# Expert loop of an encoder block: small matmuls gathered in two places, weight rows dealt to partitions in another order

## The chip, the cores and the metric

One NeuronCore of a Trainium2 chip runs the whole kernel; the other cores are idle. The metric is the device time of one execution in microseconds (us). Engines are named as in the profile: PE is TensorE's matmul, PEld its weight load, DVE VectorE, ACT ScalarE, POOL GpSimd, SP SyncE, which issues most of the DMAs.

## The reference, cut to what matters

One encoder layer over 512 tokens of 1024 features in float32: two attention branches, a gated merge, and then a mixture of experts, which is where the change lies. Each token goes to 4 of 32 experts:

```python
def run_block(args):
    xb, e = args
    gu = xb @ w_gate_up[e] + b_gate_up[e]
    return clamped_swiglu(gu) @ w_down[e] + b_down[e]

gate, up = gu[..., :D_FF], gu[..., D_FF:]
gate = jnp.minimum(gate, 7.0)
up = jnp.clip(up, -7.0, 7.0)
hidden = (up + 1.0) * (gate * jax.nn.sigmoid(1.702 * gate))
```

`xb` holds up to 128 tokens of one expert, `w_gate_up[e]` is 1024 x 2048 and `w_down[e]` 1024 x 1024, so an expert has 12 MB of weights. The results are weighted with the router's gates and added to the tokens' rows.

## The kernel before, in words

The attention part and the router take the first 470 us and are not touched, and so are the last norm and the stores. From there the kernel goes through *items*: one item is one expert with up to 128 rows (there are 32 items here). An item's weights come in 12 *chunks* of 1 MB: chunks 0 to 3 are the gate columns, 4 to 7 the up columns, 8 to 11 the down matrix, each chunk 256 rows of 1024 numbers. `expert_src` (line 295) lays the 256 rows on 128 partitions, two to a partition. Before the change partition p holds rows 2p and 2p+1.

float32 products are made from two rounded parts: ACT copies a chunk to its high part (`ex_split_hi`, line 656), DVE subtracts to get the low part in the chunk's own place (`ex_split_lo`, line 1032), and TensorE makes three products for each pair (`mm_split`, line 1172): high by high (line 1174), high by low and low by high (1175, 1176). One chunk is 12 matmuls of 128x512 (`weigh`, line 1413).

All engines run hand-written orders, linked by semaphores:

- SP (lines 378 to 387) loads a chunk of the next item as soon as `ex_used` says that its place has been read by TensorE.
- ACT (`act_item`, line 767) splits chunks, copies y out of PSUM with the router's weight (`rows_out`, line 757, sets `y_ready`), copies the transposed rows (`rows_hi`) and hidden values (`hidden_hi`), turns the slot products into row numbers (`index`, line 709, sets `f5_ready`), and makes the sigmoid (line 746).
- DVE (`dve_item`, line 1121) makes the one-hot rows for the slots (`serve`), the low parts, the clip of the up sum (line 1133) and the hidden values (line 1137).
- POOL (lines 492 to 502) gathers the next rows `xg` from HBM once `xt_ps` says that the last ones were transposed, and adds finished rows to `sum_rows`.
- TensorE (`pe_item`, line 1447) makes, in this order: up chunks 4 and 5, the transposes of the next item's rows (`rows_in`, line 1397), up chunks 6 and 7, the up bias; then gate chunk 0 of the next item, the slot products (`slots`, line 1386), chunk 1, the transposes of the hidden values (`hidden_T`, line 1405), chunks 2 and 3, the gate bias, the down bias; and down chunks 8 to 11.

A bias is a matmul of a bf16 table with a 0/1 column (`add_bias`, line 1425), two per bias. A slot product is four bf16 matmuls of 128x5. A transpose is a matmul with the data as weights and an identity as the moving operand, eight per item and kind. Because partition p holds rows 2p and 2p+1, the transposes must read every second column:

```python
last = t_.transpose(ps[:, 6 + k // 4, (k % 4) * CAP:(k % 4 + 1) * CAP],
                    xg[:, (k // 2) * 256 + k % 2:(k // 2 + 1) * 256:2], ident[0:CAP, 0:CAP])
```

Of the kernel before, what the change touches and what calls it, by code (L numbers as in the profile page):

```python
# [24 lines left out]
E, FF, TOPK = 32, 1024, 4  # L25
CAP = 128
# [8 lines left out]
def encoder_block(nc, x, g_mix, w_in, qa_norm, ka_norm, sink_b, w_branch_a, w_branch_b, w_out, g_ffn, w_router,  # L35
# [9 lines left out]
    with ctx:  # L45
# [3 lines left out]
        def sem(name):  # L49
            return ctx.enter_context(nc.semaphore(name))  # L50
# [44 lines left out]
        bias_tab = at("bias_tab", 190, [128, 3 * D], BF16)  # L95
# [6 lines left out]
        XT = at("XT", 96, [128, 2, KD, CAP], F32R)  # L102
# [12 lines left out]
        ident = sb("ident", [128, 128])  # L115
# [142 lines left out]
        xt_ps = sem("xt_ps")  # L258
        xt_hi = sem("xt_hi")
        xt_lo = sem("xt_lo")  # L260
        gate_ps = sem("gate_ps")
        up_ps = sem("up_ps")
        sig_done = sem("sig_done")
        glu_ready = sem("glu_ready")
        clip_ready = sem("clip_ready")
# [29 lines left out]
        def expert_src(e, c):  # L295

            q = c % 4
            if c < 8:
                w = w_gate_up[0, e, q * 256:(q + 1) * 256, (c // 4) * FF:(c // 4 + 1) * FF]
            else:  # L300
                w = w_down[0, e, q * 256:(q + 1) * 256, :]
            return w.rearrange("(p k) n -> p k n", k=2)

        def load_expert(sp, c, e):
            sp.dma_start(chunk[c][:, :].rearrange("p (k n) -> p k n", k=2), expert_src(e, c)).then_inc(expert_in[c], 16)
# [2 lines left out]
        def order(i, c, nxt):  # L308

            q = c - 4 if c in range(4, 8) else c + 4 if c < 4 else c if nxt else c - 4  # L310
            return 12 * i + 4 + q
# [194 lines left out]
        def _(act):  # L506
# [236 lines left out]
            first_split_hi(5)  # L743
            for c in (6, 7):
                ex_split_hi(0, c)
            def sigmoid(n):
                act.wait_ge(gate_ps, n)
                a.activation(sg, ps[0:CAP, 0:2, :].rearrange("p t n -> p (t n)"), ACT.Sigmoid,
                             scale=1.702).then_inc(sig_done, 1)

            a.activation(warm[:, :], eps[:, :], ACT.Sigmoid)
            sigmoid(1)
            act.wait_ge(items_ready, 1)
            last_item = act.value_load(items_i[0:1, 1:2], min_val=E - 1, max_val=E * PASSES - 1)
            act.sem_inc(y_ready, 1)
# [11 lines left out]
            def act_item(i, nxt, before=True):  # L767

                if nxt:
                    ex_split_hi(i + 1, 0)  # L770
                    ex_split_hi(i + 1, 1)
                if before:
                    rows_out(i - 1, 12 * i + 6)
                if nxt:
                    ex_split_hi(i + 1, 2)
                    rows_hi(i + 2, 0)
                    ex_split_hi(i + 1, 3)
                ex_split_hi(i, 8, nxt)
                if nxt:
                    act.wait_ge(ex_used, 12 * i + 10)  # L780
                    rows_hi(i + 2, 1)
                ex_split_hi(i, 9, nxt)
                if nxt:
                    act.wait_ge(scattered, 16 * i + ADDED)
                    index(i + 3, bass.ds((i + 3) % 4, 1))
                ex_split_hi(i, 10, nxt)
                hidden_hi(i + 1)
                ex_split_hi(i, 11, nxt)
                if nxt:
                    a.activation(warm[:, :], eps[:, :], ACT.Sigmoid)  # L790
                    ex_split_hi(i + 1, 4)
                    ex_split_hi(i + 1, 5)
                    sigmoid(i + 2)
                    ex_split_hi(i + 1, 6)
                    ex_split_hi(i + 1, 7)

# [17 lines left out]
        def _(dve):  # L814
# [306 lines left out]
            def dve_item(i, nxt):  # L1121

                if nxt:
                    dve.wait_ge(idx_done, i + 3)
                    serve(i + 3)
                    for c in range(3):
                        ex_split_lo(i + 1, c)
                    rows_lo(i + 2, 0)
                    ex_split_lo(i + 1, 3)
                else:  # L1130
                    ex_split_lo(i, 8, nxt)
                dve.wait_ge(up_ps, i + 1)
                v.tensor_scalar(hid, ps[0:CAP, 2:4, :].rearrange("p t n -> p (t n)"), 8.0, -6.0, ALU.min,  # L1133
                                ALU.max).then_inc(clip_ready, 1)
                dve.wait_ge(clip_ready, i + 1)
                dve.wait_ge(glu_ready, i + 1)
                v.scalar_tensor_tensor(out=hid, in0=sg, scalar=SILU_TOP, in1=hid, op0=ALU.min,
                                       op1=ALU.mult).then_inc(hid_ready, 1)
                if nxt:
                    rows_lo(i + 2, 1)  # L1140
                    ex_split_lo(i, 8, nxt)
                ex_split_lo(i, 9, nxt)
                hidden_lo(i + 1)
                ex_split_lo(i, 10, nxt)
                ex_split_lo(i, 11, nxt)
                if nxt:
                    ex_split_lo(i + 1, 4)
                    ex_split_lo(i + 1, 5)
                    glu(i + 2)
                    ex_split_lo(i + 1, 6)  # L1150
                    ex_split_lo(i + 1, 7)
# [16 lines left out]
        def _(pe):  # L1168
# [228 lines left out]
            def rows_in(n):  # L1397

                pe.wait_ge(gathered, n * 16)
                for k in range(KD):  # L1400
                    last = t_.transpose(ps[:, 6 + k // 4, (k % 4) * CAP:(k % 4 + 1) * CAP],  # L1401
                                        xg[:, (k // 2) * 256 + k % 2:(k // 2 + 1) * 256:2], ident[0:CAP, 0:CAP])
                last.then_inc(xt_ps, 1)

            def hidden_T(n):

                pe.wait_ge(hid_ready, n)
                for k in range(KD):
                    last = t_.transpose(ps[:, 6 + k // 4, (k % 4) * CAP:(k % 4 + 1) * CAP],  # L1409
                                        hid[:, (k // 2) * 256 + k % 2:(k // 2 + 1) * 256:2], ident[0:CAP, 0:CAP])  # L1410
                last.then_inc(hidT_ps, 1)

            def weigh(at, c, h, src, bank, fresh):

                pe.wait_ge(ex_lo, at + 1)
                q = c % 4
                for k in range(2):
                    for t in range(2):
                        last = mm_split(ps[0:CAP, bank + t, :], lambda p: src[:, p, 2 * q + k, :],
                                        lambda p: expert_w(c, h, p, k, t),  # L1420
                                        start=(fresh and q == 0 and k == 0), stop=(not fresh and q == 3 and k == 1))
                last.then_inc(ex_used, 1)
                return last

            def add_bias(e, bank, part, start):

                for t in range(2):
                    col = part * FF + t * 512
                    last = mm(ps[0:CAP, bank + t, :], pick[:, bass.ds(e, 1)].to_broadcast([128, CAP]),  # L1429
                              bias_tab[:, col:col + 512], start=start, stop=not start)  # L1430
                return last

            slots(0)
            slots(1)
# [2 lines left out]
            rows_in(1)  # L1437
            pe.wait_ge(xt_lo, 2)
            for c in range(4):
                weigh(c, c, c, XT, 0, True)  # L1440
            pe.wait_ge(bias_back, 16)
            pe.wait_ge(pick_set, 1)
            add_bias(0, 0, 0, False).then_inc(gate_ps, 1)
            pe.wait_ge(items_ready, 1)
            last_item = pe.value_load(items_i[0:1, 1:2], min_val=E - 1, max_val=E * PASSES - 1)

            def pe_item(i, nxt):

                for c in range(4, 8):
                    if c == 6:  # L1450
                        if nxt:
                            rows_in(i + 2)
                        else:
                            pe.wait_ge(gathered, (i + 2) * 16)
                            pe.sem_inc(xt_ps, 1)
                    weigh(order(i, c, nxt), c, hi_slot(c, nxt), XT, 2, True)
                add_bias(i % E, 2, 1, False).then_inc(up_ps, 1)
                if nxt:
                    pe.wait_ge(glu_ready, i + 1)
                    for c in range(4):  # L1460
                        if c == 0:
                            pe.wait_ge(xt_lo, 2 * i + 3)
                        weigh(order(i, c, nxt), c, hi_slot(c, nxt), XT, 0, True)
                        if c == 0:
                            pe.wait_ge(y_ready, i + 1)
                            slots(i + 3)
                        if c == 1:
                            pe.wait_ge(xt_lo, 2 * i + 4)
                            hidden_T(i + 1)
                    add_bias((i + 1) % E, 0, 0, False).then_inc(gate_ps, 1)  # L1470
                    pe.wait_ge(f5_ready, i + 4)
                else:
                    hidden_T(i + 1)
                    pe.wait_ge(y_ready, i + 1)
                add_bias(i % E, 4, 2, True)
                pe.wait_ge(hidT_lo, i + 1)
                for c in range(8, 12):
                    weigh(order(i, c, nxt), c, hi_slot(c, nxt), hidT, 4, False)

            with pe.Fori(0, last_item) as i:  # L1480
                pe_item(i, True)
# [40 lines left out]
```

## Time and profile before

| what | us |
|---|---|
| median of 3 runs | 1666.46 (1664.6 to 1666.61) |
| the profiled execution, whole | 1666.04 |
| its span in the profile | 1664.3 |
| TensorE busy in the span | 1597.3 (96%) |
| DVE busy | 1310.5 (79%) |
| ACT busy | 1074.0 (65%) |
| mean granted clock of TensorE | 0.98 of full speed |
| moved by DMA | 476.58 MB, 286 GB/s over the span |

The profile shows one execution. Matmuls overlap one another, so the duration of one (0.39 us for 128x512) is longer than the distance between two starts. Times in rows are us from the start of the span. "Landing" is the time from the issue of a DMA to the arrival of its last byte.

### The profile page before, as it was taken

The page shows a single profiled execution, that of the slowest core. Times are in us where ns is not written, and L with a number is a line of the kernel's source. Part 1 is how long each engine was busy: PE and PEld are TensorE (multiplying, and loading weights), DVE is VectorE, ACT ScalarE, POOL GpSimd, SP SyncE. Part 2 cuts the span into 40 slices and gives each one's busy share as a digit, 9 for nine tenths or more (in the row PEclk, how much of TensorE's full clock was granted, in tenths as well). Part 3 has the DMA queues.
Part 4 walks back from the last instruction along what each step waited for, and adds up shares of the span by engine and source line. Part 5 has one row for each costly group of instructions (what it writes and reads, how often), then busy time and mean ns, then how long its engine had stood idle before and what let it go on. Part 6 is the DMA issues. An engine that isn't in the chain of part 4 may idle for free.

```text
span 1664.3 us, 21630 instructions
## 1 busy us (share of the span) xinstructions
PE 1597.3 (96%) x7527; PEld 1266.9 (76%) x7527; DVE 1310.5 (79%) x1016; ACT 1074.0 (65%) x1113; POOL 145.5 (9%) x113
## 2 busy tenths in 40 slices
PE   7999899999969999999999999999999999999993
PEld 6788555678858888888888888888888888888882
DVE  4465464545579999998999999899999889999973
ACT  5243343422367777777777777777777777777762
POOL 6500000000010000010000001000000100000010
PEclk9999899999979999999999999999999999999997
DMA  8332000004489999999999999999999999999973
GB/s 289 120 102 76 16 1 1 1 26 177 149 343 357 381 380 381 380 373 356 381 380 381 380 380 368 362 380 381 379 383 381 360 367 382 379 381 382 378 250 126
DMA packets 114382, 476.58 MB, mean 286 GB/s; under 512 B 9704, under 2 KB 10224, under 8 KB 97872
## 3 DMA queue, kind: packets, MB, share of 16 engines
q1 hardware_dynamic: 100528, 432.83, 68.1%
q0 software_dynamic: 10224, 37.62, 8.8%
q10 hardware_dynamic: 3600, 5.73, 1.0%
q8 instruction: 19, 0.31, 0.1%
q14 instruction: 11, 0.09, 0.0%
HBM read 451.24 MB, written 24.90 MB: 286 GB/s over the span
## 4 chain that ended last, share of the span: by engine, by line
PE 94%; DVE 3%; DMA 1%; ACT 1%; issue 0%; ACTq 0%; SPq 0%; DVEq 0%; POOLq 0%
PE ps L1174 26%; PE ps L1176 26%; PE ps L1175 26%; PE ps L1429 3%; PE ps L1269 2%; PE ps L1245 2%; PE ps L1401 2%; PE ps L1409 2%; PE ps L1282 2%; PE ps L1249 1%; PE ps L1289 1%; DVE mx L898 1%; DVE split L839 1%; PE ps L1353 0%; DMA xs<-in_x 0%
## 5 line engine op out<-in xcount | busy, mean ns | idle before, releaser
L1036 DVE TENSOR_TENSOR chunk_lo<-chunk,chunk_hi 128x2048 fp32r<-128x2048 f32 x384 | 861.7, 2284 | 56.7 <-ACT chunk_hi L660 54.0
L660 ACT ACTIVATE chunk_hi<-chunk 128x2048 fp32r<-128x2048 f32 x378 | 722.9, 1914 | 136.5 <-PE ps L1176 135.5
L1174 PE MATMUL ps<-chunk_hi,XT 128*128 128x512 f32 x1024 | 413.7, 404 | 2.0 <-DVE XT L1081 2.0
L1176 PE MATMUL ps<-chunk_hi,XT 128*128 128x512 f32 x1024 | 401.1, 392 | 0.0
L1175 PE MATMUL ps<-chunk_lo,XT 128*128 128x512 f32 x1024 | 400.5, 391 | 0.0
L1174 PEld LDWEIGHTS ps<-chunk_hi,XT 128*128 128x128 f32 x1024 | 193.7, 189 | 42.7 <-DVE XT L1081 2.4
L1176 PEld LDWEIGHTS ps<-chunk_hi,XT 128*128 128x128 f32 x1024 | 192.6, 188 | 40.8
L1175 PEld LDWEIGHTS ps<-chunk_lo,XT 128*128 128x128 f32 x1024 | 193.1, 189 | 37.7
L1174 PE MATMUL ps<-chunk_hi,hidT 128*128 128x512 f32 x512 | 205.4, 401 | 1.6 <-DVE hidT L1088 1.6
L1176 PE MATMUL ps<-chunk_hi,hidT 128*128 128x512 f32 x512 | 199.8, 390 | 0.0
L1175 PE MATMUL ps<-chunk_lo,hidT 128*128 128x512 f32 x512 | 199.6, 390 | 0.0
L501 POOL DMA_INDIRECT sum_rows<-y,idx x32 | 53.8, 1681 | 1017.9 <-ACT y L764 955.6
L1174 PEld LDWEIGHTS ps<-chunk_hi,hidT 128*128 128x128 f32 x512 | 96.2, 188 | 25.3 <-issue 2.5
L1176 PEld LDWEIGHTS ps<-chunk_hi,hidT 128*128 128x128 f32 x512 | 96.1, 188 | 20.4
L1175 PEld LDWEIGHTS ps<-chunk_lo,hidT 128*128 128x128 f32 x512 | 96.2, 188 | 20.2
L839 DVE TENSOR_TENSOR split<-raw,split 128x2048 fp32r<-128x2048 f32 x14 | 40.9, 2927 | 62.2 <-ACT split L532 62.2
L480 POOL DMA_INDIRECT xg<-h_rows,idx x34 | 40.7, 1198 | 466.6 <-ACT idx L718 398.1
L724 ACT ACTIVATE XT<-ps 128x512 fp32r<-128x512 f32 x64 | 38.2, 598 | 65.0 <-PE ps L1401 41.0
L622 ACT ACTIVATE pT<-ps 128x512 f32<-128x512 f32 (+2 forms) x32 | 16.5, 517 | 88.2 <-PE ps L1269 88.2
L1133 DVE TENSOR_SCALAR hid<-ps 128x1024 f32<-128x1024 f32 x32 | 39.2, 1224 | 42.1 <-PE ps L1429 42.1
L898 DVE TENSOR_REDUCE mx<-ps 128x4 f32<-128x2048 f32 (+1 forms) x16 | 32.4, 2024 | 42.1 <-PE ps L1245 22.4
L1269 PEld LDWEIGHTS ps<-diag,probs 128*128 128x128 f32 x416 | 48.8, 195 | 7.3 <-issue 6.1
(235 smaller groups left out, 1890.5 us busy)
## 6 DMA issues: line engine op xcount, KB each, us to landing
chunk<-in_w_gate_up SPq DMA_DIRECT2D x256, 1024.0 KB, 8.9
chunk<-in_w_down SPq DMA_DIRECT2D x128, 1024.0 KB, 6.1
raw<-in_w_in SPq DMA_DIRECT2D x14, 1024.0 KB, 7.6
w_out<-in_w_out SPq DMA_DIRECT2D x4, 1024.0 KB, 5.9
xs<-in_x SPq DMA_DIRECT2D x4, 512.0 KB, 5.1
raw<-in_w_branch_a SPq DMA_DIRECT2D x2, 1024.0 KB, 5.1
raw<-in_w_branch_b SPq DMA_DIRECT2D x2, 1024.0 KB, 4.9
sum_rows<-xs ACTq DMA_DIRECT2D x4, 512.0 KB, 2.6
```

Of the source, the lines that this page charges most:

```text
L480: g.indirect_dma_start(out=xg, out_offset=None, in_=h2buf, in_offset=bass.IndirectOffsetOnAxis(ap=idx[:, col:col + 1], axis=0)).then_inc(g ...
L501: g.indirect_dma_start(out=acc, out_offset=bass.IndirectOffsetOnAxis(ap=idx[:, u:u + 1], axis=0), in_=ysb, in_offset=None, compute_op=ALU. ...
L660: a.activation(chunk_hi[hi_slot(c, nxt)][:, :], chunk[c][:, :], ACT.Copy).then_inc(ex_hi, 1)
L839: v.tensor_tensor(split[:, n % NIN_SPLIT, 1, :], raw[:, n % NIN, :], split[:, n % NIN_SPLIT, 0, :].bitcast(F32), ALU.subtract).then_inc(in ...
L898: link(v.reduce_max(mx[:, :], ps[:, 0:4, 0:w], AX.X))
L1036: v.tensor_tensor(chunk_lo[c][:, :], chunk[c][:, :], chunk_hi[hi_slot(c, nxt, first)][:, :].bitcast(F32), ALU.subtract).then_inc(ex_lo, 1)
L1133: v.tensor_scalar(hid, ps[0:CAP, 2:4, :].rearrange("p t n -> p (t n)"), 8.0, -6.0, ALU.min, ALU.max).then_inc(clip_ready, 1)
L1174: mm(dst, lhsT(0), rhs(0), start=start, stop=False)
L1175: mm(dst, lhsT(0), rhs(1), start=False, stop=False)
L1176: return mm(dst, lhsT(1), rhs(0), start=False, stop=stop)
L1269: last = mm(ps[:, 4 + m % 3, n * 128:(n + 1) * 128], probs[:, j % 2, n, c0:c0 + 128], diag[:, n, :], start=True, stop=True)
L1429: last = mm(ps[0:CAP, bank + t, :], pick[:, bass.ds(e, 1)].to_broadcast([128, CAP]), bias_tab[:, col:col + 512], start=start, stop=not start)
```

## The change

Three things. Row k*128+p of a chunk goes to partition p, which leaves each partition's two rows 128 rows apart in HBM and lets the transposes read adjacent columns. The slot products, the up bias and the row transposes stand together after up chunk 5; the gate bias, the down bias and the hidden transposes stand together after gate chunk 1, so the biases are now inside the sums. And the semaphores of the finished gate and up sums, `gate_ps` and `up_ps`, are gone: ACT and DVE wait for the count of used chunks. Ahead of the loop the first gate bias moves ahead of chunk 3.

```diff
-            return w.rearrange("(p k) n -> p k n", k=2)
+            return w.rearrange("(k p) n -> p k n", k=2)
...
-            def sigmoid(n):
-                act.wait_ge(gate_ps, n)
+            def sigmoid(used):
+                act.wait_ge(ex_used, used)
...
-                    sigmoid(i + 2)
+                    sigmoid(12 * i + 14)
...
-                dve.wait_ge(up_ps, i + 1)
+                dve.wait_ge(ex_used, 12 * i + 10)
...
-                                        xg[:, (k // 2) * 256 + k % 2:(k // 2 + 1) * 256:2], ident[0:CAP, 0:CAP])
+                                        xg[:, k * 128:(k + 1) * 128], ident[0:CAP, 0:CAP])
...
-                                        hid[:, (k // 2) * 256 + k % 2:(k // 2 + 1) * 256:2], ident[0:CAP, 0:CAP])
+                                        hid[:, k * 128:(k + 1) * 128], ident[0:CAP, 0:CAP])
...
             for c in range(4):
-                weigh(c, c, c, XT, 0, True)
-            pe.wait_ge(bias_back, 16)
-            pe.wait_ge(pick_set, 1)
-            add_bias(0, 0, 0, False).then_inc(gate_ps, 1)
+                if c == 3:
+                    pe.wait_ge(bias_back, 16)
+                    pe.wait_ge(pick_set, 1)
+                    add_bias(0, 0, 0)
+                weigh(c, c, c, XT, 0, c == 0, c == 3).then_inc(ex_used, 1)
...
-                for c in range(4, 8):
-                    if c == 6:
-                        if nxt:
-                            rows_in(i + 2)
-                        else:
-                            pe.wait_ge(gathered, (i + 2) * 16)
-                            pe.sem_inc(xt_ps, 1)
-                    weigh(order(i, c, nxt), c, hi_slot(c, nxt), XT, 2, True)
-                add_bias(i % E, 2, 1, False).then_inc(up_ps, 1)
+                def product(c, src, bank, start, stop):
+                    weigh(order(i, c, nxt), c, hi_slot(c, nxt), src, bank, start, stop).then_inc(ex_used, 1)
+
+                product(4, XT, 2, True, False)
+                product(5, XT, 2, False, False)
+                if nxt:
+                    pe.wait_ge(y_ready, i + 1)
+                    slots(i + 3)
+                    add_bias(i % E, 2, 1)
+                    rows_in(i + 2)
+                else:
+                    pe.wait_ge(gathered, (i + 2) * 16)
+                    pe.sem_inc(xt_ps, 1)
+                    add_bias(i % E, 2, 1)
+                product(6, XT, 2, False, False)
+                product(7, XT, 2, False, True)
                 if nxt:
                     pe.wait_ge(glu_ready, i + 1)
-                    for c in range(4):
-                        if c == 0:
-                            pe.wait_ge(xt_lo, 2 * i + 3)
-                        weigh(order(i, c, nxt), c, hi_slot(c, nxt), XT, 0, True)
-                        if c == 0:
-                            pe.wait_ge(y_ready, i + 1)
-                            slots(i + 3)
-                        if c == 1:
-                            pe.wait_ge(xt_lo, 2 * i + 4)
-                            hidden_T(i + 1)
-                    add_bias((i + 1) % E, 0, 0, False).then_inc(gate_ps, 1)
+                    pe.wait_ge(xt_lo, 2 * i + 3)
+                    product(0, XT, 0, True, False)
+                    product(1, XT, 0, False, False)
+                    add_bias((i + 1) % E, 0, 0)
                     pe.wait_ge(f5_ready, i + 4)
+                    pe.wait_ge(xt_lo, 2 * i + 4)
                 else:
-                    hidden_T(i + 1)
                     pe.wait_ge(y_ready, i + 1)
                 add_bias(i % E, 4, 2, True)
+                hidden_T(i + 1)
+                if nxt:
+                    product(2, XT, 0, False, False)
+                    product(3, XT, 0, False, True)
                 pe.wait_ge(hidT_lo, i + 1)
-                for c in range(8, 12):
-                    weigh(order(i, c, nxt), c, hi_slot(c, nxt), hidT, 4, False)
+                product(8, hidT, 4, False, False)
+                product(9, hidT, 4, False, False)
+                product(10, hidT, 4, False, False)
+                product(11, hidT, 4, False, True)
```

## Rows read from the trace of the kernel before

**Rows 1.** The page: chain that ended last, share of the span by engine and line.

```profile
PE 94%; DVE 3%; DMA 1%; ACT 1%; issue 0%; ACTq 0%; SPq 0%; DVEq 0%; POOLq 0%
```

**Rows 2.** Waits of PE, 520 to 1640 us: total us, times, longest us.

```profile
PE ps L1409 <- DVE hid L1137: 2.6, 1, 2.6
PE ps L1174 <- DVE hidT L1088: 1.6, 1, 1.6
```

**Rows 3.** Timeline of PE: start us, us, line, count; row transposes of two items.

```profile
1001.33 1.11 PE L1401 MATMUL ps<-ident,xg 128*128 128x128 f32 x8
...
1037.59 1.11 PE L1401 MATMUL ps<-ident,xg 128*128 128x128 f32 x8
```

**Rows 4.** Window of one item: busy us of each engine, clock, DMA share, GB/s.

```profile
1002.51:1038.78 36.27, 36.27 (x171) 29.41 (x170) 33.21 (x20) 28.00 (x25) 2.83 (x2) 1.00 1.01 375
```

**Rows 5.** Weight loads: two lines' durations (ns min/median/max); two loads from PE's timeline.

```profile
L1401 PEld LDWEIGHTS ps<-ident,xg x200: 195/209/214, 711.0 to 1582.2; 128*128 128x128 f32 x100
...
L1343 PEld LDWEIGHTS ps<-ident,xn_a x8: 138/140/142, 431.6 to 432.5; 128*128 128x128 f32 x8
...
431.42 0.19 PEld L1176 LDWEIGHTS ps<-w_out_hi,merged_T_lo 128*128 128x128 f32 x1
...
1000.87 0.19 PEld L1176 LDWEIGHTS ps<-chunk_hi,XT 128*128 128x128 f32 x1
```

**Rows 6.** Timeline of PE ahead of the loop: transposes of adjacent columns.

```profile
431.87 1.03 PE L1343 MATMUL ps<-ident,xn_a 128*128 128x128 f32 x8
...
439.90 1.07 PE L1343 MATMUL ps<-ident,xn_a 128*128 128x128 f32 x8
```

**Rows 7.** Timeline of PE: the up bias and the second product after it.

```profile
1007.77 0.60 PE L1429 MATMUL ps<-bias_tab,pick 128*128 128x512 bf16 x2
...
1008.44 0.40 PE L1175 MATMUL ps<-chunk_lo,XT 128*128 128x512 f32 x1
```

**Rows 8.** Timeline of PE: the slot products and the two products after them.

```profile
1010.95 0.25 PE L1394 MATMUL ps<-feats,shared 128*128 x4
1011.06 0.48 PE L1174 MATMUL ps<-chunk_hi,XT 128*128 128x512 f32 x1
1011.38 0.40 PE L1175 MATMUL ps<-chunk_lo,XT 128*128 128x512 f32 x1
```

**Rows 9.** Timeline of ACT and DVE: start us, us, [idle before, and what ended it].

```profile
1009.67 1.22 DVE L1137 SCALAR_TENSOR_TENSOR hid<-sig,hid 128x1024 f32<-128x1024 f32 x1
...
1011.24 0.18 ACT L712 ACTIVATE f<-ps 128x5 f32<-128x5 f32 x1 [0.87 <-PE ps L1394]
...
1016.11 1.23 DVE L1088 TENSOR_TENSOR hidT<-ps,hidT 128x1024 fp32r<-128x1024 f32 x1 [0.21 <-ACT hidT L729]
...
1020.54 1.92 ACT L660 ACTIVATE chunk_hi<-chunk 128x2048 fp32r<-128x2048 f32 x1 [0.76 <-PE ps L1176]
...
1031.59 0.68 DVE L1075 TENSOR_TENSOR shared<-iota_all,shared 128x512 bf16 x1
...
1034.52 1.12 ACT L764 ACTIVATE y<-ps,gate_c 128x1024 f32<-128x1024 f32 x1 [0.17 <-ACT gate_c L760]
```

**Rows 10.** Timeline of PE: the hidden transposes of that item.

```profile
1013.90 1.11 PE L1409 MATMUL ps<-ident,hid 128*128 128x128 f32 x8
```

**Rows 11.** DMA: 1014:1022, 1029:1036, one issue, landings 700:1600, loads 1604:1614, slices of 330:420.

```profile
DMA packets 846, 3.26 MB, mean 408 GB/s; under 512 B 50, under 2 KB 50, under 8 KB 846
...
DMA packets 391, 2.88 MB, mean 411 GB/s; under 512 B 40, under 2 KB 40, under 8 KB 40
...
1001.65 0.55 SPq L305 DMA_DIRECT2D chunk<-in_w_gate_up  x1
...
DMA to landing us min/median/max: 5.2/7.6/12.0
...
chunk<-in_w_down SPq DMA_DIRECT2D x4, 1024.0 KB, 4.9
...
GB/s 4 0 0 7 0 0 0 0 0 0 0 51 413 9 0 0 0 0 0 0 0 138 415 424 411 408 75 0 0 0 0 0 133 257 362 419 235 0 0 0
```

More of the change, by code:

```diff
@@ L260, in encoder_block @@
         xt_lo = sem("xt_lo")
-        gate_ps = sem("gate_ps")
-        up_ps = sem("up_ps")
         sig_done = sem("sig_done")
@@ L751, in _ @@
             a.activation(warm[:, :], eps[:, :], ACT.Sigmoid)
-            sigmoid(1)
+            sigmoid(6)
             act.wait_ge(items_ready, 1)
@@ L1409, in hidden_T, with weigh @@
                     last = t_.transpose(ps[:, 6 + k // 4, (k % 4) * CAP:(k % 4 + 1) * CAP],
-                                        hid[:, (k // 2) * 256 + k % 2:(k // 2 + 1) * 256:2], ident[0:CAP, 0:CAP])
+                                        hid[:, k * 128:(k + 1) * 128], ident[0:CAP, 0:CAP])
                 last.then_inc(hidT_ps, 1)
-            def weigh(at, c, h, src, bank, fresh):
+            def weigh(at, c, h, src, bank, start, stop):
                 pe.wait_ge(ex_lo, at + 1)
@@ L1420, in weigh, with add_bias @@
                                         lambda p: expert_w(c, h, p, k, t),
-                                        start=(fresh and q == 0 and k == 0), stop=(not fresh and q == 3 and k == 1))
-                last.then_inc(ex_used, 1)
+                                        start=(start and k == 0), stop=(stop and k == 1))
                 return last
-            def add_bias(e, bank, part, start):
+            def add_bias(e, bank, part, start=False):
                 for t in range(2):
                     col = part * FF + t * 512
-                    last = mm(ps[0:CAP, bank + t, :], pick[:, bass.ds(e, 1)].to_broadcast([128, CAP]),
-                              bias_tab[:, col:col + 512], start=start, stop=not start)
-                return last
+                    mm(ps[0:CAP, bank + t, :], pick[:, bass.ds(e, 1)].to_broadcast([128, CAP]),
+                       bias_tab[:, col:col + 512], start=start, stop=False)
             slots(0)
```

## The prediction

> **What bounds the kernel now.** I read the chain that ended last first: TensorE holds 94% of it, almost all of that in the split products of lines 1174 to 1176 [rows 1]. Then the waits of TensorE from 520 us on: two, both in the last item, 4.2 us together [rows 2]. So in the expert loop the matmul stream itself sets the time, with no gap. Third, the TensorE timeline of one item: it runs from one row transpose to the next, 1001.33 to 1037.59, 36.26 us [rows 3]. An item is 144 products with a pitch of 0.228 us (eleven of them between 1008.44 and 1010.95 [rows 7, 8]), 32.8 us, and, between them, the small work that the change moves: 16 transposes, 6 bias matmuls, 4 slot products, about 3.4 us. Fourth, the window over one item: the DMA share is 1.01 at 375 GB/s, DVE is busy 33.2 of 36.27 us, ACT 28.0; clock granted 1.00 [rows 4]. So the DMA engines and DVE stand close behind TensorE, and everything that I count as hidden is hidden by a small margin.
>
> **The transposes, unstrided.** Today each transpose reads every second column of `xg` or `hid` as its weights. A weight load there takes 209 ns; the same kind of transpose with adjacent columns, line 1343, loads in 140 ns [rows 5]. Loads overlap matmuls, so what counts is the group: eight strided ones last 1.11 us [rows 3], eight unstrided ones 1.03 us at 431.87 and 1.07 us at 439.90 [rows 6]. That is 0.08 or 0.04 us less per group. I take 0.08, because the group of 1.03 us follows full products, while the other follows small router matmuls. Two groups per item: 0.16 us.
>
> The rule of the Trainium skill that speaks against this (Advanced Engine Details and Errata, Memory Cachelines): a reader that hits a 16-byte line of SBUF twice runs at full rate, and a step of two float32 values does just that. By it this term would be zero and the time that of rival 2. The trace differs (209 against 140 ns [rows 5]).
>
> **The small work, gathered.** The count of bias and slot matmuls does not change; only their neighbours do. Two bias matmuls and the product behind them take 0.67 us (1007.77 to 1008.44) [rows 7], three pitches of 0.22: a bias pays no penalty for standing alone, so moving biases saves nothing. The four slot products take 0.25 us as a group, yet 0.43 us pass until the second product behind them starts (1010.95 to 1011.38) [rows 8]: 0.20 us beyond one product, of which their own pitch explains 0.11 (the next product's record starts at 1011.06). The other 0.09 us is the weight load of the next product, which four tiny matmuls cannot cover. After the change a bias stands behind the slots. Its load is of the slots' type and size, and slots follow each other every 0.03 us although each loads weights, so I take the 0.09 us as saved. Bounds: nothing saved (the bias load shows as much), or 0.1.
>
> **The sum.** 0.16 + 0.09 = 0.25 us per item, times 31 items of the loop = 7.8 us; the two groups outside the loop give 0.08 each. Together 7.9 us. The profiled execution took 1666.04 us (span 1664.3), so 1658.1; the median of the three runs is 0.4 above that execution, so 1658.5.
>
> **The waits that move.** With product 5 ending at 1001.33 as now, the first gathered group lasts about 0.11 + 0.43 + 0.87 = 1.4 us against 0.95 now, and the up sum still ends near 1008.2, since its bias is now inside.
> - The slot products, with `y_ready` ahead of them, come three chunks' products earlier, to the end of product 5. Behind this wait stands all of TensorE. The copy of y runs 1034.52 to 1035.64 [rows 9], product 5 of that item ends at 1037.59 [rows 3]: 1.9 us to spare. The one-hot rows (DVE, 1031.59, 0.68 us [rows 9]) are earlier still. Price: zero; if ACT came 2 us later, all that it is later beyond that would be paid 31 times.
> - The row transposes come 0.5 us later (slots and bias ahead of them), and with them ACT's copy of the first half and POOL's next gather; the gathered rows are wanted an item later. The second half's copy waits, as now, for product 7, some 0.45 us later.
> - `f5_ready` and `xt_lo` now stand ahead of the down bias, at about 1014.1. ACT copies f5 at 1011.24 today [rows 9], and 0.87 us of that was waiting for the slots, which will be long done: 2.7 us to spare.
> - The hidden transposes move from 1013.90 [rows 10] to about 1014.6, because both products and four biases now stand ahead of them. Their input is ready at 1010.9 (1009.67 + 1.22) [rows 9], so that wait gains cover. DVE's `hidT` subtraction at 1016.11 [rows 9] comes some 0.6 us later and ends near 1017.9; behind it stand two down subtractions. Product 8 wants it after products 2 and 3, at about 1020.9: 3 us to spare. DVE's idle time, 3 us per item [rows 4], must take the 0.6 us; it does.
> - Sigmoid and clip now wait for the last product itself, which is their bias's old place: nothing.
> - Ahead of the loop `bias_back` is wanted one set of 12 products (2.7 us) earlier. At most 2.7 us once, at least nothing; I take zero, because SP asks for the bias table ahead of the weights that item 0 needs last.
>
> **The loads.** Row k*128+p on partition p changes each 1 MB load. A gate/up load stays 256 runs of 4 KB; a down load goes from 128 runs of 8 KB to 256 of 4 KB. The stretch with 4 KB runs moves 408 GB/s, the one with 8 KB runs 411 [rows 11]: 4.2 MB of down weights per item cost 0.1 us more of DMA time. Below nothing: a `w_out` load, which already has the new order in 4 KB runs, fills one slice at 413 [rows 11], which would give 0.05 us back instead. I take +0.1. SP needs about 0.2 us more per issue (it needs 0.55 for a gate/up load [rows 11]), off the path. The cover: a load issued at 1001.65 lands at most 12.0 us later, at 1013.7, and its first reader starts at 1020.54 [rows 9, 11]: 7 us of slack. Price: zero, unless the queue falls behind item after item.
>
> **Rivals.**
> 1. *The DMA queue is the bound.* For: a share of 1.01 over the item [rows 4], and the item gets shorter. Against: a down load lands in 4.9 us when nothing follows it, and the shortest in the loop takes 5.2 [rows 11], so the queue nearly empties. With no spare at all, DMA needs 36.26 + 0.1 us against TensorE's 36.0: 0.35 us of arrears per item, 10.9 us over 31 items, of which the 7 us of slack take all but 4. Time 1662.4; with 0.2 us more of DMA time per item 1668.6.
> 2. *The stride is not what makes the weight loads long* (the loop's loads into SBUF are, say). Only the slots' 2.8 us remain: 1663.7, or 1666.5 if they do not gain either. Against: a product's weight load takes 0.19 us at 431 us and at 1001 us alike [rows 5]. This is where the skill's rule would lead.
> 3. *Slower: the new row order slows the gate/up loads.* The two rows of a partition were 8 KB apart and will be 1 MB apart. DMA has no room: if 8.4 MB per item went at 375 GB/s (the slowest whole-item rate shown [rows 4]) in place of 408, that is 1.8 us per item; 31 times, less 7 us of slack, 49 us: 1715. It decides from about 1.6% on (0.33 us per item, 31 times, less 7: +3.3 us). Against: `w_out` has this order already, its two rows 512 KB apart, at 413 GB/s [rows 11].
>
> The Trainium skill has a rule on this side (DMA: Bandwidth & Descriptors, Latency and other measured facts): copies whose partitions lie 2 or 4 MiB apart in HBM run at 164 and 103 GB/s, in place of 207 at 512 KiB. Here the partitions lie 8 KB apart and only a partition's two rows are 1 MB apart; no run here shows such a fall.
>
> **How the numbers follow.** Forecast 0.72, rivals 0.12, 0.08 and 0.08. A measurement of this kernel can tell about 0.2%, 3.3 us, from no change. Faster by more: nearly all of the forecast, a third of the first rival, some of the second: 0.77. Within: 0.13. Slower: the third and a little of the first: 0.10. The range goes from 1656 (2 us more, if the fewer changes between kinds of matmul give something) to 1665 (transposes at 0.04 and no gain at the slots, or the first rival). The third rival stays outside.
>
> **What would show it.** Right: the strided groups at 1.11 become 1.03 us with weight loads near 140 ns; slots, bias and row transposes stand together in about 1.4 us; an item takes 36.0 us; TensorE still waits only in the last item; landings rise by under 2 us. Wrong: weight loads stay near 209 ns; waits of TensorE for `y`, f5 or a `chunk_lo`; landings that grow from item to item; a 4 KB stretch well under 408 GB/s.

## The result, and the profile after

The changed kernel takes 1656.57 us (median of 5 runs, 1655.16 to 1657.93) against 1666.09 us for the kernel before on the same chip: ratio 0.9945, 95% interval 0.993 to 0.9959, so 9.5 us faster (0.55%). The forecast was 1658.5 us with a range of 1656 to 1665.

The line numbers of the changed kernel are two or three lower than before: the split products are 1172 to 1174, the slots 1392, the row transposes 1399, the hidden transposes 1407, the biases 1426. First the waits of TensorE from 515 to 1635 us (total us, times, longest us) [rows 2]:

```profile
PE ps L1172 <- DVE hidT L1086: 2.4, 1, 2.4
PE ps L1407 <- DVE hid L1135: 2.1, 1, 2.1
```

Still two waits, both in the last item: nothing that the change moved has made TensorE wait in the loop. Next its timeline: the two gathered groups, with the second product behind each, and the row transposes one item later [rows 3, 7, 8, 10]:

```profile
1008.88 1.04 PE L1426 MATMUL ps<-bias_tab,pick 128*128 128x512 bf16 x4
1009.75 1.04 PE L1407 MATMUL ps<-ident,hid 128*128 128x128 f32 x8
...
1010.86 0.39 PE L1173 MATMUL ps<-chunk_lo,XT 128*128 128x512 f32 x1
...
1032.42 0.25 PE L1392 MATMUL ps<-feats,shared 128*128 x4
1032.54 0.59 PE L1426 MATMUL ps<-bias_tab,pick 128*128 128x512 bf16 x2
1032.96 1.04 PE L1399 MATMUL ps<-ident,xg 128*128 128x128 f32 x8
...
1034.07 0.40 PE L1173 MATMUL ps<-chunk_lo,XT 128*128 128x512 f32 x1
...
1068.84 1.03 PE L1399 MATMUL ps<-ident,xg 128*128 128x128 f32 x8
```

An item is now 1068.84 - 1032.96 = 35.88 us, 0.37 or 0.38 less than before (35.89 and 36.26 as means over 29 items of the loop). Transposes last 1.03 to 1.04 us in place of 1.11. From the slots to the second product behind the group 1.65 us pass. Less one product (0.23), slots, bias and row transposes cost 1.42 us; four biases and hidden transposes cost 1.98 less a product, 1.75. Together that is 3.17 us. In the kernel before, these are the second product behind the hidden transposes, the gate and down biases, and the second product behind them:

```profile
1015.09 0.40 PE L1175 MATMUL ps<-chunk_lo,XT 128*128 128x512 f32 x1
...
1020.34 1.04 PE L1429 MATMUL ps<-bias_tab,pick 128*128 128x512 bf16 x4
...
1021.45 0.40 PE L1175 MATMUL ps<-chunk_lo,hidT 128*128 128x512 f32 x1
```

With these and [rows 3, 7, 8, 10], the same work cost 3.43 us before: row transposes 0.95, hidden transposes 0.96, up bias 0.44, slots 0.20, gate and down biases 0.88, each the distance to the second product less one product. So the groups themselves give 0.26 us. The rest, about 0.1 us, must lie in the products.

Weight loads of the row transposes (ns min/median/max) [rows 5], and one item's window (busy us of PE, PEld, DVE, ACT, POOL; clock, DMA share, GB/s) [rows 4]:

```profile
L1399 PEld LDWEIGHTS ps<-ident,xg x200: 138/140/142, 709.8 to 1571.9; 128*128 128x128 f32 x100
```

```profile
1034.07:1069.96 35.89, 35.89 (x172) 29.23 (x171) 33.20 (x20) 27.82 (x25) 5.82 (x3) 1.00 1.02 381
```

The loads are at 140 ns, and in this window DMA carries 381 GB/s in place of 375.

The gain in the loop is larger than that of the whole: 30 items from the second row transposes on give 11.2 us, the span only 8.1. In the profiled pair the loop began 1.0 us later (other runs of the same code begin up to 2 us apart), and 2.1 us were lost behind the last row transposes, 1.8 of them ahead of TensorE's last product. From the start of the last row transposes to that of the last product 60.1 us pass before (1581.51 to 1641.60) and 61.9 after (1571.29 to 1633.21). Before, with the first and the last down product:

```profile
1581.51 1.11 PE L1401 MATMUL ps<-ident,xg 128*128 128x128 f32 x8
...
1630.81 0.49 PE L1174 MATMUL ps<-chunk_hi,hidT 128*128 128x512 f32 x1 [1.59 <-DVE hidT L1088]
...
1641.60 0.39 PE L1176 MATMUL ps<-chunk_hi,hidT 128*128 128x512 f32 x1
```

And the first down product after:

```profile
1619.61 0.79 PE L1172 MATMUL ps<-chunk_hi,hidT 128*128 128x512 f32 x1 [2.44 <-DVE hidT L1086]
```

From the first to the last of these 48 products 10.8 us pass before and 13.6 after (1619.61 to 1633.21), 2.8 us more; the rest of the stretch is 1.0 us shorter. The granted clock is the reason. Stretches of 4 us of the last item, before and after (columns as above):

```profile
1626.00:1630.00 4.00, 2.83 (x10) 1.86 (x10) 3.07 (x3) 1.60 (x2) 0.00 (x0) 0.59 0.00 0
1630.00:1634.00 4.00, 3.19 (x14) 2.65 (x15) 4.00 (x3) 1.31 (x2) 0.00 (x0) 1.00 0.01 2
```

```profile
1615.00:1619.00 4.00, 1.89 (x8) 1.49 (x8) 3.17 (x3) 1.80 (x2) 0.00 (x0) 0.55 0.00 0
1619.00:1623.00 4.00, 3.39 (x8) 2.72 (x9) 4.00 (x3) 1.11 (x2) 0.00 (x0) 0.50 0.01 2
1623.00:1627.00 4.00, 4.00 (x13) 3.14 (x13) 0.88 (x1) 0.00 (x0) 0.00 (x0) 0.67 0.00 0
```

Before, the granted clock fell around the hidden transposes and the down bias (0.59) and stood at full when the down products came. After, it was still at half (1.2 of 2.4 GHz) through the first 13 or so of them: 8 start in the 3.4 us in which TensorE is busy in the second stretch, then 13 in 4 us, where at full clock 18 to 20 do (the last kernels below).

### The profile page after: what moved, and what is told of

Same layout as the page of the kernel before. It is cut to its first block, busy times and chain, and to the rows that moved or that the text cites. A ratio compares the mean times of both kernels' runs of the same rounds, so it can differ in the third digit from the quotient of the medians.

```text
span 1656.2 us, 21629 instructions
## 1 busy us (share of the span) xinstructions
PE 1586.8 (96%) x7527; PEld 1262.0 (76%) x7527; DVE 1306.5 (79%) x1016; ACT 1069.5 (65%) x1113; POOL 242.6 (15%) x113
## 4 chain that ended last, share of the span: by engine, by line
PE 94%; DVE 3%; DMA 1%; ACT 1%; issue 1%; ACTq 0%; SPq 0%; DVEq 0%; POOLq 0%
PE ps L1172 26%; PE ps L1173 26%; PE ps L1174 26%; PE ps L1426 3%; PE ps L1267 2%; PE ps L1243 2%; PE ps L1399 2%; PE ps L1407 2%; PE ps L1280 2%; PE ps L1247 1%; PE ps L1287 1%; DVE mx L896 1%; DVE split L837 1%; PE ps L1351 0%; DMA sum_rows<-y,idx 0%
## 5 line engine op out<-in xcount | busy, mean ns | idle before, releaser
L1172 PE MATMUL ps<-chunk_hi,XT 128*128 128x512 f32 x1024 | 405.1, 396 | 2.0 <-DVE XT L1079 2.0
L1174 PE MATMUL ps<-chunk_hi,XT 128*128 128x512 f32 x1024 | 399.7, 390 | 0.0
L499 POOL DMA_INDIRECT sum_rows<-y,idx x32 | 149.3, 4665 | 943.9 <-ACT y L762 884.8
L1172 PE MATMUL ps<-chunk_hi,hidT 128*128 128x512 f32 x512 | 200.5, 392 | 2.4 <-DVE hidT L1086 2.4
L1174 PE MATMUL ps<-chunk_hi,hidT 128*128 128x512 f32 x512 | 200.1, 391 | 0.0
L837 DVE TENSOR_TENSOR split<-raw,split 128x2048 fp32r<-128x2048 f32 x14 | 35.8, 2564 | 66.8 <-ACT split L530 66.8
L1086 DVE TENSOR_TENSOR hidT<-ps,hidT 128x1024 fp32r<-128x1024 f32 x32 | 39.2, 1224 | 25.0 <-ACT hidT L727 25.0
```

What stands on the lines that cost most here:

```text
L499: g.indirect_dma_start(out=acc, out_offset=bass.IndirectOffsetOnAxis(ap=idx[:, u:u + 1], axis=0), in_=ysb, in_offset=None, compute_op=ALU. ...
L837: v.tensor_tensor(split[:, n % NIN_SPLIT, 1, :], raw[:, n % NIN, :], split[:, n % NIN_SPLIT, 0, :].bitcast(F32), ALU.subtract).then_inc(in ...
L1086: v.tensor_tensor(hidT[:, 1, :, :].rearrange("p (t k) n -> p t (k n)", t=2), ps[:, 6:8, 0:4 * CAP], hidT[:, 0, :, :].rearrange("p (t k) n ...
L1172: mm(dst, lhsT(0), rhs(0), start=start, stop=False)
L1174: return mm(dst, lhsT(1), rhs(0), start=False, stop=stop)
```

## The experiments

Theory A at the start: the stride costs 0.08 us per group of eight transposes, gathering saves the load behind the slots and some slowness of the products behind each separate group, the load order costs nothing, and the clock gave back some 2 us at the end. Theory B: the new order of the loads brings the gain.

### Gathering alone

```diff
-            return w.rearrange("(k p) n -> p k n", k=2)
+            return w.rearrange("(p k) n -> p k n", k=2)
...
-                                        xg[:, k * 128:(k + 1) * 128], ident[0:CAP, 0:CAP])
+                                        xg[:, (k // 2) * 256 + k % 2:(k // 2 + 1) * 256:2], ident[0:CAP, 0:CAP])
```

(against the changed kernel; the hidden transposes likewise)

> The change without its new row order: weights laid as before (rows 2p and 2p+1 on partition p), transposes strided, small matmuls gathered in two places. Theory A (the stride costs 0.08 us per group of eight transposes; fewer separate groups save 0.09 us of weight load behind the slots and about 0.1 us of slower products behind each group; the load order costs nothing): an item of 36.05 us against 36.26 before and 35.89 after, groups of transposes at 1.11 us. Theory B (the new order of the loads brings the gain): an item of 36.25 us. Time by A about 1662 us, by B about 1666.

Measured: 1661.47 us, ratio 0.9973 (0.9963 to 0.9983). Row transposes on TensorE's timeline:

```profile
999.74 1.11 PE L1399 MATMUL ps<-ident,xg 128*128 128x128 f32 x8
...
1035.80 1.11 PE L1399 MATMUL ps<-ident,xg 128*128 128x128 f32 x8
```

An item of 36.06 us, with strided groups of 1.11 us: gathering alone gives 0.20 us. As theory A said.

### The row order alone, and the stride alone

Row order alone, against the kernel before:

```diff
-            return w.rearrange("(p k) n -> p k n", k=2)
+            return w.rearrange("(k p) n -> p k n", k=2)
...
-                                        xg[:, (k // 2) * 256 + k % 2:(k // 2 + 1) * 256:2], ident[0:CAP, 0:CAP])
+                                        xg[:, k * 128:(k + 1) * 128], ident[0:CAP, 0:CAP])
```

> The kernel before with the new row order alone: row k*128+p on partition p, transposes unstrided, small matmuls where they were. Theory A: groups of transposes at 1.03 us, an item of 36.09 us, time about 1661 us; the products behind each group as slow as before. Theory B: an item of 35.9 us, as after.

Stride alone: the same diff without its first change.

> The kernel before with unstrided transposes but the old row order of the weights, so the rows that meet in the products are the wrong ones (the output is left wrong in the expert part; the work is the same). Theory A: the stride alone makes the difference, an item of 36.09 us as with the new row order, down loads landing in about 6.0 us as before (against 6.9 us with 4 KB runs). Theory B: no gain without the new order of the loads, 36.25 us.

Measured: 1659.49 us, ratio 0.9958 (0.9943 to 0.9973), with the new order; 1659.87 us, 0.9959 (0.9944 to 0.9974), with the old. TensorE with the row order alone: transposes, the second product behind, the last product ahead of the up bias, and the next item's transposes:

```profile
1000.25 1.03 PE L1401 MATMUL ps<-ident,xg 128*128 128x128 f32 x8
...
1001.35 0.40 PE L1175 MATMUL ps<-chunk_lo,XT 128*128 128x512 f32 x1
...
1006.35 0.39 PE L1176 MATMUL ps<-chunk_hi,XT 128*128 128x512 f32 x1
...
1036.29 1.03 PE L1401 MATMUL ps<-ident,xg 128*128 128x128 f32 x8
```

And with the stride alone, two up biases an item apart:

```profile
1005.12 0.61 PE L1429 MATMUL ps<-bias_tab,pick 128*128 128x512 bf16 x2
...
1041.16 0.61 PE L1429 MATMUL ps<-bias_tab,pick 128*128 128x512 bf16 x2
```

Both items are 36.04 us. So the order of the loads does nothing for the time, and theory B falls. The gain, 0.22 us, is more than the 0.16 us by which two groups are shorter. The rest stands behind the groups: from the second product to the last before the bias 5.00 us pass here (1001.35 to 1006.35); in the kernel before, 5.03 for the same 22 steps:

```profile
1002.51 0.40 PE L1175 MATMUL ps<-chunk_lo,XT 128*128 128x512 f32 x1
...
1007.54 0.39 PE L1176 MATMUL ps<-chunk_hi,XT 128*128 128x512 f32 x1
```

Strided transposes thus also slow the products behind them, by 0.03 us per group; theory A had expected these products to be as slow as before. It was also wrong on the landings of the down loads. Their median is 6.0 us in the kernel before and with the row order alone, 6.5 with the stride alone, 7.0 with gathering alone and 6.9 in the changed kernel. So the 6.9 us go with the gathering, and not with runs of 4 KB.

### The slots alone again

```diff
-                    pe.wait_ge(y_ready, i + 1)
-                    slots(i + 3)
                     add_bias(i % E, 2, 1)
...
                     product(0, XT, 0, True, False)
+                    pe.wait_ge(y_ready, i + 1)
+                    slots(i + 3)
```

> The changed kernel with the slot products (and their wait for y) back behind gate chunk 0, alone between products; all else as after. My prediction's step (0.09 us of weight load is exposed only where a product follows the slots): an item of 35.98 us against 35.89. With a cost of slower products behind each separate group as well: 36.00 to 36.01 us. Rival (the slots cost the same anywhere): 35.89 us.

One run, 1660.96 us. TensorE: slots and second product, twice, and between them the up bias, behind which the row transposes come, and the second product behind those:

```profile
1006.63 0.26 PE L1392 MATMUL ps<-feats,shared 128*128 x4
...
1033.13 0.60 PE L1426 MATMUL ps<-bias_tab,pick 128*128 128x512 bf16 x2
...
1034.68 0.40 PE L1173 MATMUL ps<-chunk_lo,XT 128*128 128x512 f32 x1
...
1042.65 0.25 PE L1392 MATMUL ps<-feats,shared 128*128 x4
...
1043.08 0.40 PE L1173 MATMUL ps<-chunk_lo,XT 128*128 128x512 f32 x1
```

An item of 36.02 us (36.01 as a mean over the loop), 0.12 or 0.13 more than after. Alone the slots cost 0.43 less a product, 0.20 us, as before. In the gathered group they cost 1.65 - 1.55 = 0.10 us. So the exposed weight load is 0.10 us, and the 0.02 or 0.03 us beyond it I put down to slower products behind the additional group. This kernel also shows what the biases gain: here they stand with the transposes, and with the row order alone, where an item takes 36.04 us, they stand apart. That is 0.03 us.

### The gate bias apart

```diff
                     product(0, XT, 0, True, False)
+                    half_bias((i + 1) % E, 0)
                     product(1, XT, 0, False, False)
-                    add_bias((i + 1) % E, 0, 0)
...
                     product(2, XT, 0, False, False)
+                    half_bias((i + 1) % E, 1)
                     product(3, XT, 0, False, True)
```

(`half_bias` is one of the two matmuls of the gate bias.)

> The changed kernel with the two matmuls of the gate bias set apart, one alone behind gate chunk 0, one alone behind gate chunk 2; all else as after. My prediction's step (a bias pays nothing for standing alone): an item of 35.89 us as after. Theory A, second part (each separate group slows some eight products behind it, 14 to 40 ns in all): 35.92 to 35.97 us.

One run, 1663.15 us. Row transposes an item apart; and one lone bias with the second and the twelfth product behind it:

```profile
999.89 1.04 PE L1399 MATMUL ps<-ident,xg 128*128 128x128 f32 x8
...
1016.06 0.39 PE L1431 MATMUL ps<-bias_tab,pick 128*128 128x512 bf16 x1
...
1016.51 0.39 PE L1173 MATMUL ps<-chunk_lo,XT 128*128 128x512 f32 x1
...
1018.82 0.39 PE L1174 MATMUL ps<-chunk_hi,XT 128*128 128x512 f32 x1
...
1035.91 1.03 PE L1399 MATMUL ps<-ident,xg 128*128 128x128 f32 x8
```

An item of 36.02 us: two lone bias matmuls cost 0.13 or 0.14 us, more than either side expected. At the bias itself little is to be seen: 0.45 us to the second product. Behind it ten steps take 2.31 us, 0.231 each, where undisturbed products of the changed kernel have a pitch of 0.227 (18 steps in the last item):

```profile
1629.13 0.39 PE L1174 MATMUL ps<-chunk_hi,hidT 128*128 128x512 f32 x1
...
1633.21 0.39 PE L1174 MATMUL ps<-chunk_hi,hidT 128*128 128x512 f32 x1
```

That is 0.04 us behind each, 0.08 of the 0.13 us; where the rest lies these rows do not show. Why the products behind a foreign matmul are slower for a while stays open. Nor is this the price of the biases in the kernel before, where none stood alone: two stood together, and four. Behind its up bias eleven steps take 2.51 us [rows 7, 8], 0.01 or 0.02 more than undisturbed.

### The last item: the bias back, and the waits filled

```diff
                 else:
+                    hidden_T(i + 1)
                     pe.wait_ge(y_ready, i + 1)
-                add_bias(i % E, 4, 2, True)
-                hidden_T(i + 1)
+                    add_bias(i % E, 4, 2, True)
```

(in the last item alone; the items of the loop keep the bias ahead of the transposes)

> The changed kernel, but in the last item alone the down bias stands behind the hidden transposes again, as before the change. Theory A (in the last item TensorE waits 2.4 us for hidT in place of 1.6, its clock falls to half for 10 us in place of 3, and that gave back some 2 us): the wait for hidT 1.6 us, the half clock some 3 us, the same item of 35.89 us, and 2 to 3 us less than the changed kernel, 1654 us. Rival (the fall of the clock depends on when the last item comes, not on the wait's length): half clock of 10 us again, time as after, 1656.5 us.

Measured: 1655.63 us (1654.8 to 1657.11), not told apart from the changed kernel. The wait for hidT is 1.6 us as expected, yet the clock stayed at half for some 7 us, the stretch with the first products among them:

```profile
1613.00:1617.00 4.00, 1.89 (x10) 1.02 (x10) 3.96 (x4) 2.23 (x2) 0.00 (x0) 0.71 0.00 0
1617.00:1621.00 4.00, 3.82 (x9) 3.05 (x10) 4.00 (x3) 0.69 (x2) 0.00 (x0) 0.50 0.01 2
1621.00:1625.00 4.00, 4.00 (x17) 3.24 (x17) 0.45 (x1) 0.00 (x0) 0.00 (x0) 0.94 0.00 0
```

So the length of that one wait does not settle it. Nor does the place of the down bias. With the row order alone and with the stride alone TensorE does the same work in the last item, the bias in its old place and the waits as before (2.6 and 1.6 us). Yet in the profile of the first the clock is at half for the first down products, and in that of the second at full:

```profile
1625.00:1629.00 4.00, 3.58 (x9) 2.89 (x10) 4.00 (x3) 0.93 (x2) 0.00 (x0) 0.52 0.01 2
```

```profile
1624.00:1628.00 4.00, 3.58 (x16) 2.96 (x17) 4.00 (x3) 0.92 (x2) 0.00 (x0) 1.00 0.01 2
```

So executions of the same work in the last item differ in how long the clock stays at half, and one profile of the kernel before cannot show that the change made it longer.

The next kernel leaves no wait to speak of. It fills both with matmuls that nobody reads; it was run beside the changed kernel itself.

```diff
+            def fill(count, e):
+                for n in range(count):
+                    mm(ps[0:CAP, n % 2, :], pick[:, bass.ds(e, 1)].to_broadcast([128, CAP]),
+                       bias_tab[:, 0:512], start=True, stop=True)
...
+                    pe.wait_ge(glu_ready, i + 1)
                 add_bias(i % E, 4, 2, True)
+                if not nxt:
+                    fill(9, i % E)
                 hidden_T(i + 1)
+                if not nxt:
+                    fill(10, i % E)
```

> The changed kernel, with 9 and 10 bias matmuls into the unused gate sums put into the two waits of the last item, so that TensorE does not stand idle there (they add work whose result nobody reads). Theory A (idle time in the last item brings the clock down, and the slow products behind it give back 2 to 3 us): granted clock 1.00 throughout the last item, the stretch from the last row transposes to TensorE's last product 59.5 to 60 us in place of 62.3, and 2 to 3 us less time than the changed kernel on the same chip. Rival (the clock falls there for another reason): half clock again, the added matmuls only cost, time not below the changed kernel's.

> The changed kernel once more, beside the others on the same chip: an item of 35.89 us; in the last item waits of 2.1 and 2.4 us, with half clock behind them for 7 to 10 us. Median 1656.5 us.

Measured: filled 1653.48 us (1653.12 to 1654.51), ratio 0.9927 (0.9914 to 0.9941); the changed kernel beside it 1654.73 us (1654.23 to 1656.28), 0.9937 (0.9923 to 0.995). Last item, filled; then the changed kernel again:

```profile
1614.00:1618.00 4.00, 3.47 (x19) 1.88 (x19) 3.96 (x4) 2.48 (x2) 0.00 (x0) 1.00 0.01 2
1618.00:1622.00 4.00, 4.00 (x18) 3.29 (x19) 4.00 (x2) 0.43 (x2) 0.00 (x0) 1.00 0.00 0
```

```profile
1617.00:1621.00 4.00, 3.53 (x9) 2.82 (x10) 4.00 (x3) 0.98 (x2) 0.00 (x0) 0.55 0.01 2
1621.00:1625.00 4.00, 4.00 (x20) 3.27 (x19) 0.74 (x1) 0.00 (x0) 0.00 (x0) 1.00 0.00 0
```

With the waits down to 0.2 and 0.3 us the clock stays at full in this execution. Over the whole kernel the mean granted clock of the five executions is 0.981 to 0.983 filled and 0.979 to 0.980 in the changed kernel beside it. From the start of the last row transposes to that of TensorE's last product 58.3 us pass (1570.41 to 1628.73), against 60.3 in the changed kernel beside it (1569.39 to 1629.71) and 61.9 in its first profile (1571.29 to 1633.21). So the same code, with the same waits of 2.1 and 2.4 us, lost 1.6 us more in one execution than in another. The medians say 1.25 us less for the filled one, short of the 2 to 3 us expected, and the two intervals overlap. It has the lowest median of the kernels here. The changed kernel itself came out 1.8 us below the 1656.5 us expected of it.

## Why the prediction was right

The direction, the place and the mechanism were right; the sum came out too small because it left out the products behind a small matmul, and one thing at the end was missed.

- *The transposes, unstrided.* Weight load 209 to 140 ns and group 1.11 to 1.03 us, as worked out. The stride alone is enough for it, whatever the load order (36.04 us both ways). "What counts is the group" was too narrow: 0.03 us per group in the products behind was missed, so 0.16 us was forecast and 0.22 measured.
- *"A bias pays no penalty for standing alone, so moving biases saves nothing."* This step was wrong, by 0.03 us per item (36.04 with the row order alone, 36.01 with only the slots still apart). I looked at the bias and the one product behind it, where little is lost, and not at the ten behind that. Two bias matmuls set apart one by one cost more, 0.13 us, but the kernel before had none such.
- *The slots.* 0.09 us forecast for the load that shows, 0.10 measured, by the same reading: the load of the next product shows behind four tiny matmuls and not behind a bias. With the products behind it is 0.12 or 0.13.
- *The sum.* 0.25 us per item forecast, 0.37 measured: stride 0.22 (36.26 to 36.04), biases 0.03 (to 36.01), slots 0.12 (to 35.89). Gathering with strided transposes gave 0.20, more than these 0.15; that both shorten the same slow products is my reading and was not tried.
- *The total was near in part by luck.* 31 items at 0.37 us make 11.5 us, 3.7 more than the 7.8 of the sum. The medians differ by 9.5 us and the profiled pair by 8.1, close to the 7.9 forecast; in that pair, a later start of the loop and the clock at the end took back most of what the sum had missed.
- *The edges.* A gain of 0.08 us each was forecast. Instead the stretch from the last row transposes to the last product, 60.1 us in the one profile of before, took 61.9 and 60.3 us in the two of the changed kernel, and half clock on the down products is the cost. The down bias no longer stands in the second wait, so the wait has grown from 1.6 to 2.4 us. Whether the change lengthened the half clock stays open: it also met the kernel with the bias back and one of two kernels whose last item is as before.
- *The waits that move.* All held. In ACT's timeline y ends at 1030.48, 1.9 us before the slots want it; f5 no longer waits for the slots. DVE's hidT subtraction stands behind a longer idle stretch, 0.76 us in place of 0.21 [rows 9], as the 0.6 us later transposes said, and TensorE does not wait for it in the loop:

```profile
1029.36 1.12 ACT L762 ACTIVATE y<-ps,gate_c 128x1024 f32<-128x1024 f32 x1 [0.17 <-ACT gate_c L758]
...
1041.84 0.18 ACT L710 ACTIVATE f<-ps 128x5 f32<-128x5 f32 x1
...
1047.77 1.22 DVE L1086 TENSOR_TENSOR hidT<-ps,hidT 128x1024 fp32r<-128x1024 f32 x1 [0.76 <-ACT hidT L727]
```

- *The loads.* No price, as forecast. Landings of an expert's chunk (the last number is the longest) in the loop of the changed kernel [rows 11]:

```profile
DMA to landing us min/median/max: 5.9/7.3/10.7
```

The longest fell from 12.0 to 10.7, so the queue does not fall behind: rival 1 did not come. Rival 2 is refuted by the kernel with the stride alone. Rival 3 is refuted by 381 GB/s over an item and by two equal items with either order. My 0.2 us more per issue on SP was wrong (below), and on no path.
- *The Trainium skill's rule on 16-byte lines* (Advanced Engine Details and Errata, Memory Cachelines) would have given no gain from a step of two float32 values. Here such a step lengthens a weight load from 140 to 209 ns and costs 0.22 us per item; for weight loads of TensorE the measurement decides against it.

## What to carry to other kernels

Read a small matmul's cost from its start until the pitch behind it is back at its undisturbed value, not until the next product: a lone bias cost 0.04 us more in the ten products after it, and strided transposes 0.03. Where several kinds of small matmuls cut into one long stream, put them together, with one long enough to cover the next weight load behind the shortest ones, and lay data out so that a transpose reads adjacent columns. And look at the last pass by itself: behind the waits there the clock fell in every profile but one, that of the kernel whose waits were filled with work of no use. What it costs differs between executions.

## What the runs showed that I had not expected

- SP's issue of a gate/up load takes 0.37 us with the new row order and took 0.54 with the old; a down load takes 0.37 and took 0.33. The row order alone brings both. The gate/up loads after the change (ns min/median/max; before, the median was 543):

```profile
L303 SPq DMA_DIRECT2D chunk<-in_w_gate_up x196: 372/373/373, 707.0 to 1578.0; - x196
```

- POOL's scatter of finished rows, 1.68 us as a mean before, takes 4.83 us in the loop of the changed kernel (page: 4665 ns as a mean of all 32). It hides, since the next is 36 us away. It goes with the gathering: in the loop the mean is 1.72 us with the row order alone and with the stride alone, and 2.59 with gathering alone. What lengthens it is not shown.
